# A gated DeltaNet core rewritten: from two groups per loop pass and a separate sample stage to a three-stage round order

## The reference, cut to what matters

```python
def chunk_gated_delta(q, k, v, beta, g, s0):
    ...
    decay = jnp.exp(jnp.where(causal, gc[..., :, None] - gc[..., None, :], -jnp.inf))
    kb = k * beta[..., None]
    vb = v * beta[..., None]
    lower = jnp.where(strict, jnp.einsum('bhnid,bhnjd->bhnij', kb, k) * decay, 0.0)
    a_mat = eye + lower
    t_mat = lax.linalg.triangular_solve(a_mat, jnp.broadcast_to(eye, a_mat.shape),
                                        left_side=True, lower=True, unit_diagonal=True)
    u = jnp.einsum('bhnij,bhnje->bhnie', t_mat, vb)
    w = jnp.einsum('bhnij,bhnjd->bhnid', t_mat, kb * jnp.exp(gc)[..., None])
    attn = jnp.einsum('bhnid,bhnjd->bhnij', q, k) * decay
    def step(state, inp):
        qi, ki, ui, wi, gi, ai = inp
        v_new = ui - jnp.einsum('bhcd,bhde->bhce', wi, state)
        o = (jnp.einsum('bhcd,bhde->bhce', qi * jnp.exp(gi)[..., None], state)
             + jnp.einsum('bhcj,bhje->bhce', ai, v_new))
        ...
        state = state * jnp.exp(g_last)[..., None, None] + jnp.einsum('bhcd,bhce->bhde', k_dec, v_new)
        return state, o
```

## Time and profile before

| what | value |
|---|---|
| median of 3 runs (lowest to highest) | 3052.87 us (3047.98 to 3055.24) |
| profiled execution, its own time | 3050.74 us |
| its span, first to last instruction | 3049.0 us |
| PE, DVE, ACT, POOL busy (share of the span) | 89%, 40%, 27%, 32% |
| granted PE clock, mean | 0.918 |
| chain that ended last: PE, DVE, DMA | 82%, 9%, 3% |

### The profile page before, as it was taken

How to read it: one execution, slowest core, us unless ns; L and a number is a source line. 1 busy time by engine, 2 the same in 40 slices (tenths; PEclk the granted TensorE clock), 3 DMA queues, 4 the chain that set the end, 5 groups by cost and what they waited for, 6 DMA issues and landing times.

```text
span 3049.0 us, 51275 instructions
## 1 busy us (share of the span) xinstructions
PE 2700.5 (89%) x20143; PEld 2581.6 (85%) x20143; DVE 1225.6 (40%) x2204; ACT 831.0 (27%) x1296; POOL 971.8 (32%) x453
## 2 busy tenths in 40 slices
PE   7999983899998999997999889989776659899997
PEld 7999972899997999996899879889764349799996
DVE  4312328531334321326777354454331342531334
ACT  4412221441323432224443211111100142431221
POOL 2343322233342433332334322231211323243331
PEclk9999986999999999999999989999855579999998
DMA  3232320132231232331245510100114322223231
GB/s 108 86 93 79 97 72 14 56 90 83 87 91 56 83 92 81 88 86 49 70 128 156 187 49 21 41 21 21 44 45 114 116 86 85 60 85 87 83 96 58
DMA packets 424267, 239.39 MB, mean 79 GB/s; under 512 B 15462, under 2 KB 411983, under 8 KB 423622
## 3 DMA queue, kind: packets, MB, share of 16 engines
q1 hardware_dynamic: 413523, 233.37, 26.2%
q10 hardware_dynamic: 10670, 5.01, 0.6%
HBM read 208.18 MB, written 30.52 MB: 78 GB/s over the span
## 4 chain that ended last, share of the span: by engine, by line
PE 82%; DVE 9%; DMA 3%; ACT 2%; issue 1%; SPq 1%; POOL 1%; DVEq 0%; ACTq 0%; POOLq 0%
PE acc L684 64%; PE aux L805 2%; PE aux L816 1%; PE acc L816 1%; PE acc L805 1%; DVE y L1326 1%; PE aux L820 1%; PE acc L820 1%; PE aux L693 1%; DVE x L1329 1%; PE acc L883 1%; PE aux L883 1%; DVE rpost L1304 1%; PE acc L911 1%; DMA out_delta_sample_dram<-Ss 1%
## 5 line engine op out<-in xcount | busy, mean ns | idle before, releaser
L548 POOL TENSOR_TENSOR wlo<-wraw,whi 128x1024 fp32r<-128x1024 f32 (+2 forms) x305 | 788.7, 2586 | 1417.6 <-ACT whi L1042 1417.6
L684 PE MATMUL acc<-hlo,whi 128*128 128x272 f32 x3600 | 1042.5, 290 | 0.0
L684 PE MATMUL acc<-hhi,whi 128*128 128x272 f32 x3600 | 1039.9, 289 | 2.4 <-POOL wlo L548 2.4
L684 PE MATMUL acc<-hhi,wlo 128*128 128x272 f32 x3600 | 1035.0, 287 | 0.0
L684 PEld LDWEIGHTS acc<-hhi,whi 128*128 128x128 f32 x3600 | 676.3, 188 | 10.6 <-issue 7.2
L684 PEld LDWEIGHTS acc<-hhi,wlo 128*128 128x128 f32 x3600 | 677.2, 188 | 0.5
L684 PEld LDWEIGHTS acc<-hlo,whi 128*128 128x128 f32 x3600 | 675.2, 188 | 0.3
L1042 ACT ACTIVATE whi<-wraw 128x1024 fp32r<-128x1024 f32 (+2 forms) x305 | 340.0, 1115 | 387.5 <-PE acc L684 350.1
L684 PE MATMUL acc<-hidhi,whi 128*128 128x272 f32 x1408 | 406.3, 289 | 12.4 <-DVE hidlo L1351 12.4
L684 PE MATMUL acc<-hidhi,wlo 128*128 128x272 f32 x1408 | 407.7, 290 | 0.0
L684 PE MATMUL acc<-hidlo,whi 128*128 128x272 f32 x1408 | 404.9, 288 | 0.0
...
## 6 DMA issues: line engine op xcount, KB each, us to landing
wraw<-in_w_ffn_gate_dram SPq DMA_DIRECT2D x88, 512.0 KB, 3.8
wraw<-in_w_ffn_up_dram SPq DMA_DIRECT2D x88, 512.0 KB, 3.9
...
wraw<-in_dn_w_in_dram SPq DMA_DIRECT2D x48, 512.0 KB, 4.2
wraw<-in_dn_w_out_dram SPq DMA_DIRECT2D x16, 512.0 KB, 4.0
Ss<-in_state_delta_dram SPq DMA_DIRECT2D x16, 512.0 KB, 6.9
out_delta_sample_dram<-Ss SPq DMA_DIRECT2D x16, 512.0 KB, 5.9
...
```

The costliest lines, as they stand in the source:

```text
L548: pool.tensor_tensor(wlo[s][:, 0:nk, 0:width], wraw[s][:, 0:nk, 0:width], whi[s][:, 0:nk, 0:width].bitcast(F), ALU.subtract).then_inc(w_lo ...
L684: last = pe.matmul(acc[s][0:width, hf, 0:HT], w[s][:, k, 0:width], a[:, k0 + k, cols(hf)], start=(n == 0), stop=(n == 3 * nk - 1))
```

## The change

The core is written anew on all engines; the projections, the FFNs and the pooling mixer are left as they are.

- A round r (PAIRS = 8) takes 8 heads of a chunk, as before two groups of four. Ten passes `for r in range(PAIRS + 2)` are written out, and a pass holds three stages of three different rounds: key products, decay and base inverse of round r (`A`), the inverse's levels of round x = r-1 (`X`), and state products, outputs and state step of round t = r-2 (`Rr`).
- The inverse starts from 16 x 16 blocks in place of 2 x 2. DVE makes them (`base_inverse`, `base_inverse_top`: 19 small instructions on 64 partitions). For that the products M go to DRAM (`m_d`) and come back as blocks (`Mg`, 64-byte pieces), and the inverse blocks go to DRAM (`t_d`, `u_d`) and come back as full tiles (`Tm`, `U`). Then PE needs two levels and one last step (`top_y`, `top_u`) where it needed six levels.
- The decays are broadcast from a DRAM scratch (`gc_d`) by SP, masked by POOL and exponentiated by ACT head by head; two products and two transposes of a round go away with that.
- The samples have four groups of four heads, two per pass pair: in even passes from r = 2 the 32 products with the states (`sample_state`), behind the prompt's last products; in odd passes from r = 3 the rest (`sample_step`), between them. Their base blocks run with round 0.
- The core's buffers lie where `y`, `wraw`, `whi`, `wlo` lie. So the first weights of the output projection are loaded behind the core (`load_out(0, k)`) and split during the norm.
- At the kernel's beginning DVE clears a buffer and SP writes it to `t_d`, `u_d`, `us_d` (2.25 MB) ahead of the first FFN weights.

Part of the diff, only what the text below speaks of:

```diff
+            for d in (t_d, u_d):
+                sp.dma_start(d.rearrange("(p n) -> p n", p=P), zero[:]).then_inc(scratch_out, 16)
+            sp.dma_start(us_d.rearrange("(p n) -> p n", p=P), zero[:, 0:4 * PITCH // P]).then_inc(scratch_out, 16)
...
+        def blocks(a, first, n):
+
+            return bass.AP(a.tensor, first * PITCH, [[16 * (P + 1), 8 * n], [P, 16], [1, 16]])
...
+                for r in range(PAIRS + 2):
+                    if r < PAIRS:
+                        sp.wait_ge(m_c, 2 * r + 2)
+                        sp.dma_start(tiles(m_d, 8 * (r % 2), 8), M[r % 2][:, :, :]).then_inc(m_st, 16)
...
+                    if r + 1 < PAIRS:
+                        load_kq(r + 1)
+                        sp.wait_ge(att_c, 2 * r + 2)
+                        load_decay(r + 1, gd, gd_in)
+                    if r < PAIRS:
+                        sp.wait_ge(m_st, 16 * (r + 1))
+                        sp.dma_start(Mg[0:64, :, :], blocks(m_d, 8 * (r % 2), 8)).then_inc(m_g, 16)
...
+                    if r < PAIRS:
+                        load_v(r)
+                    if 2 <= r - 1 < PAIRS:
+                        if r - 1 >= 3:
+                            sp.wait_ge(sd_c, r - 3)
+                            sp.wait_ge(qd_c, r - 3)
+                        load_decay(r - 1, eg, eg_in)
+                    if r == 0:
+                        load_state(0)
+                        load_state(1)
+                    if r >= 3 and r % 2 == 1:
+                        store_state((r - 3) // 2)
+                    if r in (4, 6):
+                        load_state((r - 4) // 2 + 2)
+                    if r < PAIRS:
+                        sp.wait_ge(b_step, 19 * (r + 1))
+                        if r >= 2:
+                            sp.wait_ge(tu_in, 32 * (r - 1))
+                        for d, b in ((t_d, Tb), (u_d, Ub)):
+                            sp.dma_start(blocks(d, 8 * (r % 2), 8), b[0:64, :, :]).then_inc(tu_st, 16)
...
+                    if r < PAIRS:
+                        sp.wait_ge(tu_st, 32 * (r + 1))
+                        if r >= 1:
+                            sp.wait_ge(y_ps, 6 * r)
+                        if r >= 2:
+                            sp.wait_ge(vn_ps, 2 * r - 2)
+                        for dst, d in ((Tm, t_d), (U[r % 2], u_d)):
+                            sp.dma_start(dst[:, :, :], tiles(d, 8 * (r % 2), 8)).then_inc(tu_in, 16)
...
+                    if r >= 2:
+                        store_out(r - 2)
...
+                for k in range(2):
+                    load_out(0, k)
...
+                for r in range(PAIRS + 2):
+                    t = r - 2
+                    if t >= 2:
+                        hs = slice(8 * (t % 2), 8 * (t % 2) + 8)
+                        pool.wait_ge(eg_e, t - 1)
...
+                                           eg[:, :, :].rearrange("p (k v) i -> p k v i", v=2), ALU.mult).then_inc(qd_c, 1)
+                        pool.wait_ge(s_c, 2 * (t - 1) + 2)
+                        pool.tensor_tensor(Sd[:, :, :], S[:, hs, :], eg[:, :, P - 1:P].broadcast_to([P, 8, P]), ALU.mult).then_inc(sd_c, 1)
+                    if r + 1 < PAIRS:
+                        pool.wait_ge(gd_in, 16 * (r + 2))
+                        pool.tensor_tensor(gd[:, :, :], gd[:, :, :], mask, ALU.add).then_inc(gd_m, 1)
...
+                    if r >= 2 and r % 2 == 0:
+                        g = r // 2 - 1
+                        last = egs[:, g, :].rearrange("p (h b t) -> p h b t", h=4, b=NB)
+                        pool.wait_ge(KQ_ps, g + 1)
                         for h in range(4):
-                            j = 4 * q + h
-                            pool.wait_ge(sn_s, i * 16 + 2 * j)
-                            last_cols = GS[q].eg[:, h, :].rearrange("p (b t) -> p b t", b=NB)[:, :, NS - 1:NS]
-                            pool.tensor_tensor(Sds[h % 2][:], Ss[q][:, h, :, :], last_cols.broadcast_to([P, NB, P]), ALU.mult)\
-                                .then_inc(sd_s, 1)
+                            pool.tensor_tensor(Ss[g % 2][:, h, :, :], Ss[g % 2][:, h, :, :],
+                                               last[:, h, :, NS - 1:NS].broadcast_to([P, NB, P]), ALU.mult).then_inc(ssd_c, 1)
+                    if r >= 3 and r % 2 == 1:
+                        g = (r - 3) // 2
+                        pool.wait_ge(vns_c, g + 1)
+                        if g:
+                            pool.wait_ge(dss_ps, 8 * g)
+                        pool.tensor_tensor(vnm[:, :, :], vns[:, :].unsqueeze(1).broadcast_to([P, NB, P]),
+                                           own_seq.unsqueeze(2).broadcast_to([P, NB, P]), ALU.mult).then_inc(vnm_c, 1)
...
+                    if Rr:
+                        outputs(t, 0)
+                        state_step(t, 0)
+                    if X:
+                        level_ut(x, 1, 0)
+                        level_ut(x, 1, 1)
+                    if f is not None:
+                        sample_step(f, 2)
+                        sample_step(f, 3)
+                    if Rr:
+                        outputs(t, 1)
+                        state_step(t, 1)
+                    if g is not None:
+                        sample_state(g, (0, 1))
+                    if X:
+                        top_y(x, 0)
+                        top_y(x, 1)
+                    if f is not None:
+                        sample_step(f, 4)
+                        sample_step(f, 5)
+                    if g is not None:
+                        sample_state(g, (2, 3))
+                    if X:
+                        top_u(x, 0)
+                        top_u(x, 1)
+                    if f is not None:
+                        sample_step(f, 6)
+                        sample_step(f, 7)
...
+                    if r + 1 < PAIRS:
+                        decay(r + 1)
+                    if Rr:
+                        new_values(t, 0)
...
+            def base_inverse(r, n):
...
+                dve.wait_ge(m_g, 16 * (r + 2))
+                if r >= 1:
+                    dve.wait_ge(tu_st, 32 * r)
...
+                dve.tensor_scalar(at(Ub, 1, (68, 4), (17, 3)), at(Mg, 1, (68, 4), (17, 3)), -1.0, None, ALU.mult).then_inc(b_step, 1)
...
+            def base_inverse_top(r, n):
...
+                    if X:
+                        level_y(x, 1, 0)
+                        level_y(x, 1, 1)
+                    if A:
+                        base_inverse(r, 96 if r == 0 else 64)
+                    if f is not None:
+                        sample_step(f, 0)
+                        sample_step(f, 1)
+                    if X:
+                        level_ut(x, 1, 0)
+                        level_ut(x, 1, 1)
+                    if Rr:
+                        state_step(t, 0)
+                    if f is not None:
+                        sample_step(f, 2)
+                        sample_step(f, 3)
+                    if A:
+                        base_inverse_top(r, 96 if r == 0 else 64)
+                    if f is not None:
+                        sample_step(f, 4)
+                        sample_step(f, 5)
+                    if Rr:
+                        state_step(t, 1)
+                    if f is not None:
+                        sample_step(f, 6)
+                        sample_step(f, 7)
...```

The places in the written order that matter below. On DVE, in the middle of a round, between the decay products and the state; before, one level of the six (`Y`, `U`, `T` are inverse tiles, `q` groups as 0 and 1):

```order
L1468 TENSOR_TENSOR Y_128_0<-acc,cst 128x128x2 [waits y_ps_0]
L1468 TENSOR_TENSOR Y_128_1<-aux,cst 128x128x2 [waits y_ps_1]
L1477 TENSOR_TENSOR U_0<-U_0,acc 128x128x2 [waits ut_ps_0]
L1480 TENSOR_TENSOR T_0<-T_0,acc 128x128x2
L1477 TENSOR_TENSOR U_1<-U_1,aux 128x128x2 [waits ut_ps_1]
L1480 TENSOR_TENSOR T_1<-T_1,aux 128x128x2
```

1347 lines of the change are left out of this document (722 added, 625 removed).

## The result

The changed kernel takes 2814.57 us (median of 4 runs, 2806.20 to 2817.79) where the kernel before takes 3052.15: a ratio of 0.9217, 95% interval 0.9202 to 0.9231. The profiled execution took 2817.79, its span is 2816.0. The forecast was 2842, range 2780 to 2960.

The account below looks back on a forecast made before the run. PE, mostly on the inverse, was taken to bound the prompt's rounds. Core 673 to 451 us, 222 less, plus 11 outside it: 3050.7 becomes 2840, and 2 for the median gives 2842; range 2780 to 2960.

Parts of the forecast that it names:

- the two chains: Even passes end with PE's query products waiting for POOL's qd, odd ones with a wait for loads of Tm and U.
- start to the first level product: Core's start, 56 us: 17 before M, 8 samples' pieces, 8 M through DRAM, 6 base, states' loads ahead, 9 blocks.
- pass 1: Core's second stretch, 27 us: levels partly at low clock, then the next base and blocks.
- passes 3, 5, 7: Odd passes, 50 us each: PE and DVE 39, states' store 1.7, blocks' stores 3.5, loads 5.6.
- passes 4, 6, 8: Even passes, 48 us each, ended by POOL's state multiplications, then qd, then PE's query products.
- norm, beginning: Outside the core: weight loads and roundings ahead of the norm, +6 us; zeros ahead of the first weights, +5.
- 22, 13, 10.2 and 2.6: Even pass: levels to last state step 22 us, state products with top_y 13, POOL 10.2, query products 2.6.
- named signs: Among them: first FFN product 4 to 6 us later; profile chain names DVE and DMA instead of PE's level lines.
- The 2887: Sum in us if 64-byte pieces doubled M's blocks and the two stores, an odd pass about 5 us longer.
- A: Rival: PE's clock does not fall in its gaps, core 384 us, so 2775; chance 0.15.
- B: Rival: all matrix work at 1.2 GHz, core 612 us, so 3003, half-way case 2920; chance 0.22 with that case.
- C: Rival: DRAM way on SP's queue sets the pass, 7.6 ns a piece more, slower; 3110 at 12 ns; chance 0.05.

Follow-up runs that it names:

- double_store: Changed kernel with SP storing the inverse's blocks twice, first to an unused place in DRAM; 2821.28 us, ratio 0.9244.
- kernel with SP's new order: Changed kernel with SP's four sample-state stores moved behind the stores and loads of the inverse's blocks; 2815.51 us, ratio 0.9232.
- five: Kernel with three orders, plus scratch zeros written behind the first two weight loads and first two sample-state loads issued in passes 1 and 2; 2770.85 us.
- kernel with three orders: Changed kernel with SP's sample stores behind the blocks' transfers, POOL's state multiplications behind next qd and Sd, ACT's decays behind new values; 2786.45 us.
- kernels with POOL's or ACT's order alone: Changed kernel with either POOL's sample-state multiplications behind the next qd and Sd (2819.29 us) or ACT's next decays behind the new values (2809.11 us).
- 128-row products and the three orders: Kernel with three orders, its sample-step state products made with 128 rows instead of 32, using zeroed tiles; 2763.54 us, ratio 0.9057.
- few_state: Kernel with three orders, sample-state products cut from 32 of 8 columns a pass to 4 of 64; 2750.02 us, ratio 0.9013.

## Why the prediction was right, and where it was off

The direction, the range and the two chains held. The forecast was 27 us above the median: 22 from its terms (211 us forecast between the two profiled runs, 233 measured), and 5 because the median lies 3.2 below this profiled run and lay 2 above that of before.

| term | forecast | measured |
|---|---|---|
| start to the first level product | 56 | 50.0 |
| pass 1 | 27 | 34.0 |
| pass 2 | 42 | 40.9 |
| passes 3, 5, 7 | 3 x 50 | 49.6, 41.0, 44.5 |
| passes 4, 6, 8 | 3 x 48 | 44.6, 45.1, 46.2 |
| pass 9 to the last landing | 32 | 35.7 |
| norm, beginning | +6, +5 | +5.6, +4.0 |

(The start is counted from 1.2 us behind the last input product, as 1740 stood to it before.) The core is 431.7 by these terms where 451 was forecast: the odd passes are 15 of the 19 us, the even ones 8 and pass 2 is 1, pass 9 took 4 of it back, and the start's 6 and pass 1's 7, with opposite signs, cancel, which was luck.

**The even passes.** The steps were 22, 13, 10.2 and 2.6; pass 4 has 20.3, 12.5, 9.9 and 1.9. The order of the chain was right, and 13 for the state products, half at each clock, was close to the measured 12.5. That the clock would fall between the halves was assumed there, not derived.

**The odd passes** are the term that was mis-sized most. The chain was right: double_store lengthened its waits alone, and in the kernel with SP's new order they went. The steps of pass 5: 24.2 us to top_y where 28 was charged, 6.8 from there to DVE's last addition where 11 was, 4.8 for the blocks' way out against 1.7 + 3.5, 5.3 for the loads against 5.6. So the DRAM part was right to 0.7 us, and the error is PE's part. I charged 3 us of low clock behind a wait, 1.33 for a 512-column product, and 1.8 each for top_y and top_u. Pass 5 began without such a wait and had a clock of 0.91; at full clock two of these products took 1.91, and top_y and top_u 1.07 each. In pass 3 the 6.56 us behind the decays stand against that, and its way to top_y took 33.1; the forecast had let this chain be covered and called 3 to 5 us a pass open. It showed in one pass of three. So the term's error is not the same in every pass, and another execution can move it: the passes of one form lie 9 us apart by the clock and this wait.

**Pass 1** was 7 too short. I had it "partly at low clock"; after the 17.4 us wait it ran at 0.55, the level's groups of four products 1.71 us behind each other instead of 0.90. **The start** was 6 too long: M's way with the samples' pieces took 11.7 us (1762.14 to 1773.81) where 8 and 8 were charged, and from the base's end to the first product were 12.5 (1781.60 to 1794.07) where 8 and 9 were. With the states' loads moved (five) the second of these took 8.7, so the loads cost about 4 there, not 8. Against that stand 18.1 for 17 and 7.8 for 6 in the other steps.

**Signs and sums.** Two of the named signs did not come as written. The first FFN product starts 2.8 us later (36.10 to 38.86), not 4 to 6; the +4.0 of the table is counted at the last input product. And the page's chain names DVE for 7% (9% before) and DMA for 3% as before: it still names level products (L930, L937, L940, 1% each), and new in it are POOL's multiplications of states, the decays' load and the blocks' store. In the sums and readings, the steps of an odd pass up to DVE's end give 38.4, not 39. The 2887 counts 5 us in nine places, though by the forecast's own reading only some of the passes end there. And 12 ns a piece more would give 3174, not 3110. That small pieces land in about the time of large ones is not in the earlier trace rows, which have no transfer of that size in larger pieces.

**The rivals.** A (2775) and B (3003) were both about the clock. The core's 0.73 lies between them, inside the 0.6 to 0.85 that was named. The Trainium skill, TensorE: Matmul & The Clock Gate, HAM oscillation, on which B leaned, tells of waits for data behind which the next stretch starts at the low clock. The trace agrees as to the falls: behind the 17.4 us wait for U pass 1 runs at 0.50, and behind the 3.29 us before pass 6 the first sixteen records take 3.68 us instead of 1.90. But most of the low clock in the even passes follows no wait at all, as the stretches of the kernel with three orders show. C is settled by double_store: at most 1.0 ns a piece more, against 7.6.

**What was argued and not shown.** Why the clock came back 11 us after the wait in pass 3 of the changed kernel and only after 34 to 40 us in the kernels with POOL's or ACT's order alone, with the same products in the same order on PE, stays open. With 128-row products and the three orders it came back 6 us after the wait for vnm in pass 3. But the 32-row products are not needed for a long low clock. In pass 1 there are none, nor any of 8 columns, and behind the 17.4 us wait PE is busy without a break at 0.50 until the key products:

```profile
1794.07:1818.28 24.21, 24.21 (x129) 23.97 (x129) 9.41 (x29) 3.58 (x11) 3.58 (x2) 0.50 0.32 94
```

Every kernel here has that stretch (pass 1 takes 34 to 36 us in each), and no run takes it apart. And few_state changes the columns of a product together with the number of products and of weight loads, so which of these brings the clock down is not shown.
